# Weight tiles in steps of 576 bytes, operand rows of 4160 bytes, and low parts 32 bytes further on

## The reference, cut to what matters

```
h = rms_norm(x, ffn_norm_g[l])
ff = jax.nn.silu(jnp.einsum("btd,df->btf", h, w_gate[l])) * jnp.einsum("btd,df->btf", h, w_up[l])
x = x + jnp.einsum("btf,fd->btd", ff, w_down[l])

def swiglu(h, w1, w3, w2):
    return (jax.nn.silu(h @ w1) * (h @ w3)) @ w2
```

## Time and profile before

| | |
|---|---|
| median of the runs | 3608.73 us |
| the profiled execution's own time | 3607.34 us |
| its span, first to last instruction | 3605.6 us |
| PE busy | 3520.8 us, 98% |
| weight loads (PEld) busy | 2933.4 us, 81% |
| DVE, ACT, POOL busy | 1465.4, 963.0, 1132.6 us |
| DMA, mean of the span | 60 GB/s |
| mean granted clock of TensorE | 0.991 |

### The profile page before, as it was taken

The page is one execution under the profiler, slowest core; times in us unless marked ns, Lnnn a source line. Parts: engine busy times, 40 slices in busy tenths (PEclk is TensorE's granted clock), DMA queues, the critical chain, the costliest instruction groups (busy, mean ns, idle before and its releaser), DMA issues.

```text
span 3605.6 us, 52857 instructions
## 1 busy us (share of the span) xinstructions
PE 3520.8 (98%) x20076; PEld 2933.4 (81%) x20076; DVE 1465.4 (41%) x2553; ACT 963.0 (27%) x1684; POOL 1132.6 (31%) x1499
## 2 busy tenths in 40 slices
PE   8999899999999999999999999999999999999998
PEld 6787778888888889899999878887777888888886
DVE  7865545211111263322122563737876521111214
ACT  5254533111111142110111332215663411111112
POOL 4433045222223252222222532300025532222323
PEclk9999899999999999999999999999999999999999
DMA  3113022111111121111111332110024311111113
GB/s 125 41 49 86 1 100 82 51 54 42 51 40 54 48 81 49 46 47 47 47 47 45 99 101 69 42 35 33 33 92 149 94 57 54 47 44 50 47 45 102
DMA packets 81556, 218.51 MB, mean 61 GB/s; under 512 B 18928, under 2 KB 19056, under 8 KB 80880
## 3 DMA queue, kind: packets, MB, share of 16 engines
q1 hardware_dynamic: 61792, 173.35, 15.5%
q10 hardware_dynamic: 19600, 42.88, 3.3%
HBM read 195.67 MB, written 19.46 MB: 60 GB/s over the span
## 4 chain that ended last, share of the span: by engine, by line
issue 61%; POOL 24%; PE 9%; DVE 4%; ACT 1%; POOLq 1%; DMA 0%; DVEq 0%; ACTq 0%; SPq 0%
POOL w_lo L572 24%; PE acc L731 2%; PE acc L732 2%; PE acc L733 2%; DVE cv_acc L1747 2%; PE acc L1281 0%; PE acc L1276 0%; POOLq L576 0%; PE acc L1398 0%; DVE ssq L680 0%; PE acc L1340 0%; PE acc L1415 0%; DVE tmp L692 0%; DVE cvo L1838 0%; PE acc L1407 0%
## 5 line engine op out<-in xcount | busy, mean ns | idle before, releaser
L572 POOL TENSOR_TENSOR w_lo<-w_raw,w_hi 128x256 fp32r<-128x256 f32 (+3 forms) x1480 | 1111.8, 782 | 2352.4 <-ACT w_hi L542 2351.9
L731 PE MATMUL acc<-h_hi,w_hi 128*128 128x512 f32 (+1 forms) x3520 | 1301.4, 370 | 15.8 <-issue 4.7
L732 PE MATMUL acc<-h_lo,w_hi 128*128 128x512 f32 (+1 forms) x3520 | 1300.8, 370 | 0.0
L733 PE MATMUL acc<-h_hi,w_lo 128*128 128x512 f32 (+1 forms) x3520 | 1295.7, 368 | 0.0
L731 PEld LDWEIGHTS acc<-h_hi,w_hi 128*128 128x128 f32 x3520 | 662.7, 188 | 143.2 <-issue 13.3
L732 PEld LDWEIGHTS acc<-h_lo,w_hi 128*128 128x128 f32 x3520 | 662.0, 188 | 118.3 <-issue 1.9
L733 PEld LDWEIGHTS acc<-h_hi,w_lo 128*128 128x128 f32 x3520 | 663.3, 188 | 114.9
L542 ACT CAST w_hi<-w_raw 128x1024 fp32r<-128x1024 f32 (+3 forms) x370 | 346.3, 936 | 1205.1 <-PE acc L733 1190.5
L1012 DVE TENSOR_TENSOR ff_hi<-tmp,acc 128x512 f32 (+3 forms) x154 | 94.6, 614 | 1098.6 <-PE acc L733 1066.6
L731 PE MATMUL acc<-ff_hi,w_hi 128*128 128x512 f32 (+1 forms) x1232 | 447.2, 363 | 6.1 <-POOL w_lo L572 3.4
L732 PE MATMUL acc<-ff_lo,w_hi 128*128 128x512 f32 (+1 forms) x1232 | 443.2, 360 | 0.0
(11 more groups left out here) (377 smaller groups left out, 3010.4 us busy)
## 6 DMA issues: line engine op xcount, KB each, us to landing
w_raw<-in_ffn_w_dram SPq DMA_DIRECT2D x94, 512.0 KB, 3.5
w_raw<-in_w_in_dram SPq DMA_DIRECT2D x60, 512.0 KB, 3.5
w_raw<-in_w_out_dram SPq DMA_DIRECT2D x32, 512.0 KB, 3.5
w_raw<-in_ffn_w_dram SPq DMA_DIRECT2D x48, 320.0 KB, 2.8
w_raw<-in_w_gate_dram SPq DMA_DIRECT2D x24, 512.0 KB, 3.5
w_raw<-in_w_up_dram SPq DMA_DIRECT2D x24, 512.0 KB, 3.5
w_raw<-in_ffn_w_dram SPq DMA_DIRECT2D x32, 384.0 KB, 3.0
gates_kept<-gstage ACTq DMA_DIRECT2D x32, 256.0 KB, 2.0
```

The costliest lines, as they stand in the source:

```text
L572: pool.tensor_tensor(w_lo[:, j, a:a + step], w_raw[:, j, a:a + step], w_hi[:, j, a:a + step].bitcast(F32), ALU.subtract).then_inc(split_do ...
L731: pe.matmul(bank, wh, rh, start=(k == 0), stop=False)
L732: pe.matmul(bank, wh, rl, start=False, stop=False)
L733: ins = pe.matmul(bank, wl, rh, start=False, stop=(k == seg.kt - 1))
```

## The change

1. `w_hi` and `w_lo` become tiles [P, 2, KD, 144]: each k has 128 floats of weights and 16 of padding, 576 bytes, 64 modulo 256. ACT's copy and POOL's subtraction go over 128-float pieces with a gap behind each in what they write (POOL also in the `w_hi` that it reads). The bytes moved are the same.
2. `h_lo` and `ff_lo` lie 32 bytes further on than a whole number of rows behind their high parts; `y_lo` and `hx_lo` do not.
3. The rows of `ff` go back from 4352 to 4160 bytes; those of `hx` go from 2048 to 2112.
4. POOL's four pieces of a slab end on whole tiles k (`PIECE_ENDS`), where for six tiles they were 192 columns each and for five 160. Their number stays.
5. To make room, `consts` loses 383 of its 1443 columns: the matrix of 1/1024 is gone (PE uses the ones and ACT scales by 1/D in the square root that it makes anyway), the matrix of 1/128 is one column, and `negstrict` is read out of `band`. Several small tiles move.

Phases (bytes modulo 256), for the chunks of CH1, where a chunk's first column adds 64:

| tile k of | before | after |
|---|---|---|
| `w_hi`, `w_lo` | 0 | 64 + 64k |
| `h_hi` | 64 + 64k | 64 + 64k |
| `h_lo` | 64 + 64k | 96 + 64k |
| `ff_hi` | 0 | 64 + 64k |
| `ff_lo` | 0 | 96 + 64k |
| `y_hi`, `y_lo` | 64 + 64k | 64 + 64k |
| `hx_hi`, `hx_lo` | 0 | 64 + 64k |

In CH2 the first chunk lies 64 bytes and the second 32 bytes lower against the weights, modulo 256, before as after; the third is as in CH1. For `ba_hi` before, the phase is 160 + 32k.

```diff
+PIECE_ENDS = {8: (2, 4, 6, 8), 6: (1, 2, 4, 6), 5: (1, 2, 3, 5), 4: (1, 2, 3, 4)}
...
     def low_pieces(self, k):
-        step = self.kt * P // LOW_PIECES
-        return -(-(k + 1) * P // step)
+        return sum(end <= k for end in PIECE_ENDS[self.kt]) + 1
...
         h_hi = place("h_hi", 0, [P, KD, L], F32R)
-        h_lo = place("h_lo", 8 * col, [P, KD, L], F32R)
-        w_raw = place("w_raw", 66560, [P, 2, KD * P])
-        w_hi = place("w_hi", 74752, [P, 2, KD * P], F32R)
-        w_lo = place("w_lo", 82944, [P, 2, KD * P], F32R)
+        h_lo = place("h_lo", 8 * col + 32, [P, KD, L], F32R)
+        w_raw = place("w_raw", 66592, [P, 2, KD * P])
+        STEP = P + 16
+        w_hi = place("w_hi", 74816, [P, 2, KD, STEP], F32R)
+        w_lo = place("w_lo", 74816 + 8 * KD * STEP, [P, 2, KD, STEP], F32R)
...
-        ff_hi = place("ff_hi", W + ff_at[0], [P, FMAX, ROW], F32R)
-        ff_lo = place("ff_lo", W + ff_at[1], [P, FMAX, ROW], F32R)
+        ff_hi = place("ff_hi", W + 8 * col, [P, FMAX, L], F32R)
+        ff_lo = place("ff_lo", W + 14 * col + 160, [P, FMAX, L], F32R)
...
-        hx_hi = place("hx_hi", W + 47104, [P, KD, 512], F32R)
-        hx_lo = place("hx_lo", W + 81920, [P, KD, 512], F32R)
+        hx_hi = place("hx_hi", W + 47168, [P, KD, 528], F32R)
+        hx_lo = place("hx_lo", W + 81984, [P, KD, 528], F32R)
...
-            act.copy(w_hi[:, j, 0:width], w_raw[:, j, 0:width]).then_inc(sem("w_high"), 1)
+            act.copy(w_hi[:, j, 0:seg.kt, 0:P], w_raw[:, j, 0:width].rearrange("p (k n) -> p k n", n=P)).then_inc(sem("w_high"), 1)
...
-                    step = width // LOW_PIECES
-                    for a in range(0, width, step):
-                        pool.tensor_tensor(w_lo[:, j, a:a + step], w_raw[:, j, a:a + step], w_hi[:, j, a:a + step].bitcast(F32),
+                    raw = w_raw[:, j, 0:width].rearrange("p (k n) -> p k n", n=P)
+                    a = 0
+                    for b in PIECE_ENDS[seg.kt]:
+                        pool.tensor_tensor(w_lo[:, j, a:b, 0:P], raw[:, a:b, :], w_hi[:, j, a:b, 0:P].bitcast(F32),
                                            ALU.subtract).then_inc(split_done, 1)
+                        a = b
...
-                    wh, wl = w_hi[:, j, k * P:(k + 1) * P], w_lo[:, j, k * P:(k + 1) * P]
+                    wh, wl = w_hi[:, j, k, 0:P], w_lo[:, j, k, 0:P]
```

More of the change, by code:

```diff
@@ L57, in _constants @@
     parts = [("ident", np.eye(P)), ("ones", np.ones((P, P))), ("upper", j <= i), ("lower", j > i),
-             ("negmask", np.where(i >= j, 0.0, NEG)), ("negstrict", np.where(i > j, 0.0, NEG))]
+             ("negmask", np.where(i >= j, 0.0, NEG))]
     prev = np.where(i > j, 0.0, NEG)
@@ L63, in _constants @@
     parts.append(("eps", np.full((P, 1), EPS)))
-    parts.append(("mean", np.full((P, P), 1.0 / D)))
     parts.append(("mean256", np.full((P, P), 1.0 / 256)))
-    parts.append(("mean128", np.full((P, P), 1.0 / 128)))
+    parts.append(("mean128", np.full((P, 1), 1.0 / 128)))
     row = np.arange(P)[:, None]
@@ L326, in param @@
             return params[:, a:a + n]
-        ROW = 1088
-        ff_at = [8 * col + 192 + v * FMAX * 4 * ROW for v in range(2)]
-        behind = ff_at[1] + FMAX * 4 * ROW
         x = place("x", W, [P, KD, L])
-        ff_hi = place("ff_hi", W + ff_at[0], [P, FMAX, ROW], F32R)
-        ff_lo = place("ff_lo", W + ff_at[1], [P, FMAX, ROW], F32R)
[L335 to L342, removed]
-        hx_hi = place("hx_hi", W + 47104, [P, KD, 512], F32R)
-        hx_lo = place("hx_lo", W + 81920, [P, KD, 512], F32R)
+        ff_hi = place("ff_hi", W + 8 * col, [P, FMAX, L], F32R)
+        ff_lo = place("ff_lo", W + 14 * col + 160, [P, FMAX, L], F32R)
+        tmp = place("tmp", W + 20 * col + 160, [P, 4, 512])
+        ssq = place("ssq", W + 20 * col + 8192 + 160, [P, L])
+        rs = place("rs", W + 21 * col + 8192 + 160, [P, L])
+        sq = place("sq", W + 22 * col + 8192 + 160, [P, 3, META + 512])
+        ahead = [place("ahead0", W + 13 * col, [P, 512]), place("ahead1", W + 13 * col + 2048, [P, 512]),
+                 place("ahead2", W + 19 * col + 160, [P, 512])]
+        ahead_u = [place(f"ahead_u{k}", W + 20 * col + 160 + 2112 * k, [P, META + 512]) for k in range(3)]
+        hx_hi = place("hx_hi", W + 47168, [P, KD, 528], F32R)
+        hx_lo = place("hx_lo", W + 81984, [P, KD, 528], F32R)
         tmp0 = place("tmp0", W + 47104, [P, 4, 512])
@@ L347, in build_program @@
         sq0 = place("sq0", W + 33280, [P, 3, 512])
-        rs0 = place("rs0", W + 102720, [P, 2, 512])
-        ssq0 = place("ssq0", W + 106848, [P, 2, 512])
+        rs0 = place("rs0", W + 103008, [P, 2, 512])
+        ssq0 = place("ssq0", W + 39424, [P, 2, 512])
         kT = place("kT", W, [P, HEADS, SEQ])
@@ L366, in build_program @@
         cvo = place("cvo", W + 98592, [P, 2, SEQ])
-        lgt = place("lgt", W + 98592, [P, SEQ])
+        lgt = place("lgt", W + 98880, [P, SEQ])
         dsq = place("dsq", W + 106784, [P, SEQ])
@@ L618, in pe_first_mean @@
             pe.wait_ge(sem("x_added"), (KD - 1) * (c + 1))
-            pe.matmul(acc[:, 6 + c, :], const("mean"), ssq0[:, c, :], start=True, stop=True, skip_group_check=True)\
+            pe.matmul(acc[:, 6 + c, :], ones, ssq0[:, c, :], start=True, stop=True, skip_group_check=True)\
               .then_inc(sem("x_ms"), 1)
@@ L641, in root @@
                 act.wait_ge(sem("x_ms"), c + 1)
[L642 removed]
+                act.activation(rs0[:, c, :], acc[:, 6 + c, :], ACT.Sqrt, bias=const("eps"), scale=1.0 / D).then_inc(sem("sd_mix1"), 1)
             act.wait_ge(sem("params_full"), 16)
@@ L752, in pe_mean @@
             for p, (c0, w) in enumerate(turn_parts(name, half)):
-                pe.matmul(acc[:, 6 + half + p, 0:w], const("mean"), ssq[:, c0:c0 + w], start=True, stop=True)\
+                pe.matmul(acc[:, 6 + half + p, 0:w], ones, ssq[:, c0:c0 + w], start=True, stop=True)\
                   .then_inc(sem("ms_full"), 1)
@@ L1062, in pe_meta @@
             pe.wait_ge(sem("meta_summed"), 1)
-            pe.matmul(acc[:, 6, 0:META], const("mean"), meta_sum, start=True, stop=True).then_inc(sem("meta_ms"), 1)
+            pe.matmul(acc[:, 6, 0:META], ones, meta_sum, start=True, stop=True).then_inc(sem("meta_ms"), 1)
         def act_meta(act, i):
@@ L1071, in act_meta @@
                 act.wait_ge(sem("meta_ms"), 1)
-                act.activation(meta_rs, acc[:, 6, 0:META], ACT.Sqrt, bias=const("eps")).then_inc(sem("meta_sd"), 1)
+                act.activation(meta_rs, acc[:, 6, 0:META], ACT.Sqrt, bias=const("eps"), scale=1.0 / D).then_inc(sem("meta_sd"), 1)
         def dve_meta(dve, own, i):
@@ L1108, in pe_fin @@
             for half in range(2):
-                pe.matmul(acc[:, 6 + half, :], const("mean"), ssq[:, fin_columns(half)], start=True, stop=True)\
+                pe.matmul(acc[:, 6 + half, :], ones, ssq[:, fin_columns(half)], start=True, stop=True)\
                   .then_inc(sem("fin_ms"), 1)
@@ L1363, in shared @@
                         for hd in range(HEADS):
-                            ins = pe.matmul(sums[:, HEADS * n + hd:HEADS * n + hd + 1], osq[v // 2][:, hd, blk(n)], const("mean128")[:, 0:1],
+                            ins = pe.matmul(sums[:, HEADS * n + hd:HEADS * n + hd + 1], osq[v // 2][:, hd, blk(n)], const("mean128"),
                                             start=False, stop=True, skip_group_check=True)
```

15 lines of the change are left out of this document (8 added, 7 removed).

## The result

The changed kernel is slower: 3626.57 us median (3623.01 to 3630.52, 5 runs) against 3607.74 us (3606.95 to 3608.97) of the kernel before, a ratio of 1.0049 with a 95% interval of 1.0036 to 1.0061. The forecast was 3561, so its sign was wrong, and the median lies 0.6 us above the upper end of the range, 3626.

A forecast was written before the change was run, and what follows sets the result against it. PE, busy 3520.8 of 3605.6 us, bounds the kernel through its matmuls' start-to-start distances. 3607.3 - 48.2 (44.2 and 4.0) + 0.5 = 3559.6, with the median 1.4 us above: 3561 us; range 3546 to 3626.

The forecast's parts named there:

- That `h` is slow by phases modulo 256: Up stages: `h` takes 231.7 ns a matmul against 226.7 for `ff`, differing in byte address modulo 256.
- Rival C: Phases irrelevant: operand rows or `ff`'s place count, or `ff` eats gains on `h`; 3600 to 3616 us, chance 0.10.
- The first term, 8832 matmuls down by 5.0 ns, -44.2 us: Matmuls of `h`, `y` and L2184 to L2186, 512 columns: weights stepping alike bring 231.7 to 226.7 ns, 44.2 us less.
- The 264 columns, -4.0 us: The 3 x 832 matmuls of 264 columns come down by at most 1.6 ns each, 4.0 us.
- L732's 32 bytes at price 0: L732, low operand 32 bytes on: price between 0 and 13 ns, 0 to 49.7 us over 3824 matmuls; taken as 0.
- `ff` unchanged: Down stages: 2640 `ff` matmuls of 512 columns stay as they are; going to 231.7 ns would lose 13.2 us.
- ACT, POOL, the constants, `hx`: Copy and subtraction with gaps, fewer constants, `hx` matmuls: nothing, or small waits of 3 us at most; +0.5 us taken.
- The side remark on loads of 8 columns: Short loads bring neighbours no closer than 226.7 ns, so the price hangs on where the two streams begin, not load length.
- D: A jump costs, not a distance: `h` stays, `ff` goes to 231.7, 3624 us; 3639 if all three pay; chance 0.18.
- A: Rival as summed: 3561 us, 3555 to 3572 with some 264-column matmuls unchanged and small waits; chance 0.44.
- B: L732 pays for its 32 bytes: 3586 us at 6.5 ns, 3578 at 4.4, 3611 at 13; chance 0.22.
- What the prediction feared above all: In the big matmuls: equal phases with the load that runs count, not those with one's own weights; no size given.

The follow-up runs named there:

- steady_fit: Against rest_only: `h` rows paired at stride 8448, low parts 160 bytes on, low weights 128 on, all phases constant over k; 3573.68 us, ratio 0.9904.
- rest_only: Changed kernel with weights, `h` and `ff` back at the earlier phases; smaller constants, piece ends and tile-wise copies stay; 3608.12 us, ratio 0.9998.
- ff_rows: Layout before the change (as rest_only), only `ff` rows 4160 bytes instead of 4352, low part 128 on; 3620.46 us, ratio 1.0033.
- steady_misfit: Against steady_fit: low weights at phase 0 from the high ones instead of 128, all still constant over k; 3618.84 us, ratio 1.0034.
- lo_back: Changed kernel without the 32 bytes ahead of `h_lo` and `ff_lo`, both streams still stepping by 64; 3617.86 us, ratio 1.0024.
- m1_phases: Separate program, no kernel: series of 48 matmuls in threes at set phases and steps; at 512 columns 226.5 ns at phase 0, 231.7 with equal steps.
- m2_sweep: Separate program, no kernel: 177 series of 72 matmuls in threes, 512 columns, wider choice of phases and low-part offsets; lowest distance 226.7 ns.

## Why the prediction was wrong, point by point

**What bounds the kernel: right.** PE's start-to-start distance, with nothing waiting. The gain of steady_fit lies there: 39.4 us on `h`, of which some 5 are lost again in the other work.

**That `h` is slow by phases modulo 256: right**, and rest_only, ff_rows and steady_fit show it from three sides. Rival C does not hold: the same program moves by 45 us between steady_fit and steady_misfit with one address. With it falls what the prediction drew from the Trainium skill, "SBUF — State Buffer", section "Who interferes with whom", where PE never waits on anyone: that addresses are free. Whether the load and the running matmul take anything from each other, no run here shows. One argument for phases was weak, though. The prediction read threes of 0.70, 0.70, 0.69 and 0.69 us as the step from k to k+1; steady_misfit has the same uneven threes with no step at all.

**The first term, 8832 matmuls down by 5.0 ns, -44.2 us: wrong, and this is the step that failed.** It took "distance to one's own weights is 0" from `ff` as what makes 226.7. But `ff` had three properties at once: distance 0, no step, and low parts at the same phase as the high ones. The earlier trace rows can't tell the first two apart, as `h` lacked both. With distance 0 restored and the step left (lo_back) `h` has 231.6 instead of 231.8, `y` in the changed kernel 231.6 instead of 231.7, and the series with equal steps has the 231.7 of unequal ones. Measured on `h` in the changed kernel: +4.0 us in place of -44.2.

**The 264 columns, -4.0 us: a small part of it.** -1.1 on `h`. The series show why the rows at this width say little: 121.4 ns without a step and 121.1 with one.

**L732's 32 bytes at price 0: wrong.** The low bound came from `ff` at 264 columns, where distances of 64 and 32 cost nothing; but at that width the series show next to no price for a step either, so that row could not bear on 512 columns. The count was off too: `y` has no 32 bytes, so that 3696 matmuls pay and not 3824. Between lo_back and the changed kernel the 32 bytes are worth 10.6 us over 3 x 3696 matmuls of 512 columns, 2.9 ns for each of the 3696 L732: inside the range of 0 to 13, not at its lower end. If the price is spread over all three matmuls it is 1.0 ns for each, where the earlier trace rows gave 4.4. In series where all else is constant, the same 32 bytes cost 6.7 ns (m1_phases) or 5.0 (m2_sweep) on each of three: the price hangs on what else steps, so it was no term of a sum at all.

**`ff` unchanged: wrong, and the larger loss.** The prediction priced its going to 231.7 at 13.2 us and did not take it; measured 12.7 + 1.2 for both widths. It said in so many words that `ff` gives up constant phases for the pattern of `h`; the row that showed what constant phases are worth was the earlier trace rows itself.

**ACT, POOL, the constants, `hx`: right.** rest_only is 0.9998 (0.9989 to 1.0008). POOL's pieces take 860 ns and PE waits 19.8 us for them instead of 20.8.

**The side remark on loads of 8 columns: half right.** Neighbours of short loads do come no closer than 226.7. But it concluded that the price hangs only on where the two streams begin, and the series with 8 weight columns has 231.1 with all at phase 0, where loads of 128 have 226.7. So prices read from short loads, as in the earlier trace rows, need not hold for loads of 128 columns.

**The rivals.** D was the one that came: "h stays at 231.7 and ff goes there", 3624. It lies 2.6 us below the median; its mark in the profile, down stages at 2.78 us or more, is there with 2.79. What held of its reason is that both streams stepping alike are no better than one (m1_phases, lo_back). Its heading, "a jump costs, not a distance", did not hold: nearly all constant distances, which have no jump, cost 2 to 10 ns in the series, and steady_fit, where the operand's distance to the weights jumps within every three by its 160 and 128 bytes, has 227.1. And in the sum it left `h` where it was and let `ff` go to 231.7, while the 32 bytes took both to 232.4 and 232.7. That its number comes so near the median is in part luck. It had 0.18 because no row showed both streams stepping. That was a reason for an equal chance, not a small one: A rested on the same missing row. B's price is there too, but on top of D and not in its place, and not with B's mark: no one of the three distances stands 4 ns above the others (`h` 232.9, 232.2 and 232.1 in the changed kernel). What the prediction feared above all, that the phase of the load that runs is what counts, stays open: the third distance alone does not have the excess, but nothing here separates the two reads.

**The range.** With D's first form at 3624, an upper end of 3626 left no room for the 32 bytes on top of it, which B had priced at 17 to 25 us. The two were treated as alternatives where they could add.

## What to carry to other kernels

When two stages differ in pace and in several properties of their layout, give the slow stage every property of the fast one before you settle on the one that seems to matter. Here it meant to bring `h` to constant phases instead of taking them from `ff`, and it fitted into 1 KB by letting two rows share a stride. Where a stretch runs at PE's pace with nothing waiting, measure the pace in short series with the exact addresses before a layout is rewritten: a series of 48 to 72 matmuls forecast the kernel's pace to 1 ns in most stages (232.2 against 231.8 and 232.0, 229.5 against 229.8, 226.7 against 227.1; 231.7 against 232.9 in ff_rows was the worst). A sweep of 177 found the pair of offsets without which this layout loses 0.3% instead of gaining 1%.

## What the runs showed of the hardware

For matmuls of type float32r with 512 columns, 128 x 128 weights and a load for each, all at the full granted clock (2.4 GHz):

- The start-to-start distance goes from 226.7 to 236.7 ns with nothing changed from series to series but the addresses of operand and weights modulo 256; 4 bytes off are the worst found. One layout (low part 32 on, all constant) had 233.4 in one program and 231.7 in the other. All moved on alike by 32, 64 or 128 costs nothing, by 16 it is 230.0.
- Every step tried from tile to tile costs 2.7 to 7.8 ns: of the operand by 32, 64, 128 or 192, of the weights by 64, of both alike by 32, 64 or 128. Steps of the operand by 256 and 512 cost nothing.
- 226.7 is the lowest at 512 columns in any of the series; at 496, 480, 448, 384, 264 and 256 columns, all at phase 0, it is 223.4, 216.7, 202.7, 173.3, 121.4 and 120.0. Set beside the columns divided by 2.4 GHz (213.3 ns for 512), that is 13.3 ns more at 512, 384 and 256 columns, 16 to 17 more at 496, 480 and 448, and 11.4 at 264.
- Why a pair like 160 and 128 fits where 160 and 0 does not, and how the two reads meet, none of these runs shows.
